# Where a sparse mask is added: by TensorE products, or by VectorE in PSUM from a copy spread through DRAM

## What is computed

```
s = einsum('bqhd,bsd->bqhs', q_idx, k_idx) * (D_IDX ** -0.5)
score = einsum('bqh,bqhs->bqs', w_idx * (H_IDX ** -0.5), relu(s))
score = where(k_pos <= qp, score, -inf)
_, sel = lax.top_k(score, n_sel)          # n_sel = 256, one choice per query, the same for its 8 heads
...
logits = einsum('bqgrd,bqngd->bqgrn', qg, ks) * (DH ** -0.5)
logits = where(valid, logits + bias, -inf)
p = softmax(logits);  o = einsum('bqgrn,bqngd->bqgrd', p, vs)
```

## Time and profile before

| | |
|---|---|
| median of 3 runs | 2370.95 us (2370.91 to 2372.14) |
| the profiled execution's own time | 2371.31 us |
| its span on the core | 2369.8 us |
| TensorE busy | 2354.3 us (99%), 17234 instructions |
| VectorE busy | 1408.5 us (59%) |
| ScalarE busy | 919.7 us (39%) |
| GpSimd busy | 313.1 us (13%) |
| DMA | 458.70 MB, 194 GB/s over the span |
| granted TensorE clock | 0.998 of full speed |

### The profile page before, as it was taken

One profiled execution on the slowest core, in us unless ns is written; L12 is line 12 of the kernel. 1 busy time (PEld: TensorE's weight loads), 2 busy tenths in 40 slices (PEclk: granted clock), 3 DMA queues, 4 the chain that ended last, 5 costly groups with the idle time before them and its releaser, 6 DMA issues.

```text
span 2369.8 us, 44619 instructions
## 1 busy us (share of the span) xinstructions
PE 2354.3 (99%) x17234; PEld 2275.2 (96%) x17242; DVE 1408.5 (59%) x2107; ACT 919.7 (39%) x1283; POOL 313.1 (13%) x629
## 2 busy tenths in 40 slices
PE   9999999999999999999999999999999999999998
PEld 9978999999999999999999999999999999999998
DVE  6535468899987545445456655666654446666443
ACT  5334443433343444444333344333333333333432
POOL 1135110000002322333200011000000000000001
PEclk9999999999999999999999999999999999999999
DMA  7448645556658988999776544444445544444553
GB/s 242 147 131 244 178 148 180 180 169 207 205 174 262 312 291 289 301 334 312 242 264 199 187 152 148 152 154 151 151 148 154 154 151 157 154 149 151 156 149 114
DMA packets 176307, 458.70 MB, mean 194 GB/s; under 512 B 25226, under 2 KB 75002, under 8 KB 175968
## 3 DMA queue, kind: packets, MB, share of 16 engines
q1 hardware_dynamic: 142192, 370.84, 48.6%
q0 software_dynamic: 26128, 75.67, 9.9%
q10 hardware_dynamic: 7776, 9.35, 1.1%
HBM read 425.27 MB, written 27.52 MB: 191 GB/s over the span
## 4 chain that ended last, share of the span: by engine, by line
PE 96%; DVE 1%; ACT 1%; DMA 1%; issue 1%; SPq 0%; DVEq 0%; ACTq 0%
PE ps L803 88%; PE ps L1077 1%; PE ps L1030 1%; PE ps L876 1%; DMA w_raw<-in_w_in 1%; PE ps L1060 1%; ACT w_hi L1129 0%; PE ps L1000 0%; PE ps L943 0%; PE ps L992 0%; PE ps L888 0%; PE ps L979 0%; PE ps L983 0%; DVE w_lo L1406 0%; PE ps L840 0%
## 5 line engine op out<-in xcount | busy, mean ns | idle before, releaser
L1406 DVE TENSOR_TENSOR w_lo<-w_raw,w_hi 128x1024 fp32r<-128x1024 f32 (+2 forms) x630 | 750.8, 1194 | 777.1 <-ACT w_hi L1129 774.0
L803 PE MATMUL ps<-h_hi,w_hi 128*128 128x320 f32 x3696 | 1160.6, 314 | 2.4 <-DVE w_lo L1406 1.2
L803 PE MATMUL ps<-h_lo,w_hi 128*128 128x320 f32 x3696 | 1132.1, 306 | 0.0
L803 PE MATMUL ps<-h_hi,w_lo 128*128 128x320 f32 x3696 | 1125.6, 305 | 0.0
L1129 ACT ACTIVATE w_hi<-w_raw 128x1024 fp32r<-128x1024 f32 (+2 forms) x630 | 649.4, 1033 | 807.0 <-PE ps L803 774.3
L803 PEld LDWEIGHTS ps<-h_hi,w_hi 128*128 128x128 f32 x3696 | 694.5, 188 | 32.5 <-issue 25.7
L803 PEld LDWEIGHTS ps<-h_lo,w_hi 128*128 128x128 f32 x3696 | 694.6, 188 | 0.5
L803 PEld LDWEIGHTS ps<-h_hi,w_lo 128*128 128x128 f32 x3696 | 694.3, 188 | 0.0
L803 PE MATMUL ps<-y_hi,w_hi 128*128 128x320 f32 x688 | 213.3, 310 | 0.0
L803 PE MATMUL ps<-y_lo,w_hi 128*128 128x320 f32 x688 | 210.5, 306 | 0.0
L803 PE MATMUL ps<-y_hi,w_lo 128*128 128x320 f32 x688 | 209.2, 304 | 0.0
(11 more groups left out here) (329 smaller groups left out, 2070.0 us busy)
## 6 DMA issues: line engine op xcount, KB each, us to landing
w_raw<-in_w_in SPq DMA_DIRECT2D x250, 512.0 KB, 5.0
w_raw<-in_ffn_up SPq DMA_DIRECT2D x86, 512.0 KB, 4.0
w_raw<-in_ffn_gate SPq DMA_DIRECT2D x86, 512.0 KB, 3.8
w_raw<-in_ffn_down SPq DMA_DIRECT2D x80, 448.0 KB, 3.4
kpg<-in_cache_b_k SPq DMA_DIRECT2D x128, 128.0 KB, 4.5
vpg<-in_cache_b_v POOLq DMA_DIRECT2D x128, 128.0 KB, 5.1
kpg<-in_cache_a_k SPq DMA_DIRECT2D x128, 128.0 KB, 4.6
vpg<-in_cache_a_v POOLq DMA_DIRECT2D x128, 128.0 KB, 5.0
```

Source lines behind the costliest of these rows:

```text
L803: mm = mmul(bank[q][:, 0:T], wp[:, s, cols], xp[:, x.k0 + k, :], start=(x.first and k == 0 and t == 0), stop=(x.last and k == x.nk - 1 and ...
L1406: tt(w_lo[:, s, 0:n], w_raw[:, s, 0:n], w_hi[:, s, 0:n].bitcast(F32), ALU.subtract).then_inc(w_lo_done, 1)
```

## The change

The mask no longer goes through TensorE. POOL stores `m16` to a DRAM tensor `m_scr` once (at x = 1), and before each pair of mixer A loads it back into the same tile `m16`, now in the order of the logits: for each of the two requests one DMA with the eight rows of its queries repeated over eight heads (64 partitions x 2056). VectorE adds it to the logits in PSUM, one `tensor_tensor` per chunk and one for bank 6. The products with `ecur`, the constant and its load are gone, and so is TensorE's wait for `m16_done`; `lg_ps` comes right after the logits of a chunk. The page table's load now counts on `s_in` with four other constants, and its two waits are for all five. Line numbers in the changed kernel are higher (L1030 becomes L1043, L1039 becomes L1052, L803 becomes L816, L1406 becomes L1407, L1778 becomes L1786, L1795 becomes L1803, L698 becomes L711).

```diff
@@ GpSimd
-            load(ecur[:, :, :], a["c_ecur"].bitcast(BF16), s_in)
...
+            def mask_of(p):
+                for s in range(2):
+                    r = 2 * p + s
+                    row = 32 * (2 * (r % NPAIR % 2) + r // NPAIR) + TS * (r % NPAIR)
+                    load(m16[s * NS:(s + 1) * NS, :], bass.AP(m_scr.tensor, row * L, [[0, H], [L, TS], [1, L]]), m16_moved)
+
             for x in range(2 * NPAIR):
...
-                if x == NPAIR + 1:
+                if x == 1:
                     pool.wait_ge(m16_done, 1)
+                    store(m_scr, m16[:, :], m16_moved)
+                if x == 2:
+                    pool.wait_ge(m16_moved, 16)
+                    mask_of(0)
+                if x > NPAIR:
+                    pool.wait_ge(mx_done, x)
+                    mask_of(x - NPAIR)
@@ TensorE, sample(x)
-                        if mx == 1 and c < 3:
+                        if c < 3:
                             mm.then_inc(lg_ps, 1)
...
-                    if mx == 0:
-                        for c in (2 * two, 2 * two + 1):
-                            mm = mmul(bank[2 + c], ecur[:, p, :], m16[:, c * 512:(c + 1) * 512], start=False, stop=True,
-                                      skip_group_check=True)
-                            if c < 3:
-                                mm.then_inc(lg_ps, 1)
-                        if two == 1:
-                            mm = mmul(bank[6][:, 0:P], ecur[:, p, :],
-                                      m16[:, PAST:L].unsqueeze(1).to_broadcast([P, 2 * NB, TS]),
-                                      start=False, stop=True, skip_group_check=True)
...
-                if x == NPAIR:
-                    pe.wait_ge(m16_done, 1)
@@ VectorE, sample(x)
+                if mx == 0:
+                    dve.wait_ge(m16_moved, 16 + 32 * (p + 1))
                 for c in range(4):
                     dve.wait_ge(lg_ps, 4 * x + c + 1)
+                    if mx == 0:
+                        V(tt(bank[2 + c], bank[2 + c], m16[:, c * 512:(c + 1) * 512], ALU.add))
...
                     if c == 3:
+                        if mx == 0:
+                            of = bank[6][:, 0:P].rearrange("p (b t) -> p b t", t=TS)
+                            V(tt(of, of, m16[:, PAST:L].unsqueeze(1).to_broadcast([P, 2 * NB, TS]), ALU.add))
```

More of the change, by code:

```diff
@@ L170, in build @@
         w_scr = nc.dram_tensor("w_scr", [HI, NS], F32).ap()
+        m_scr = nc.dram_tensor("m_scr", [P, L], BF16).ap()
         sig_scr = nc.dram_tensor("sig_scr", [48, P, T], F32).ap()
@@ L223, in build @@
         nearN = r0("nearN", [P, 2, NPAIR * NB, TS])
-        ecur = r0("ecur", [P, NPAIR, P], BF16)
         od_at = r0.at - R
@@ L358, in build @@
         x_arrived = [sem(f"x_arrived{i}") for i in range(len(X_LOTS))]
-        g_in, ident_in, r_in, idx_in, c_in, pt_in, s_in = (
-            sem(n) for n in ("g_in", "ident_in", "r_in", "idx_in", "c_in", "pt_in", "s_in"))
+        g_in, ident_in, r_in, idx_in, c_in, s_in = (
+            sem(n) for n in ("g_in", "ident_in", "r_in", "idx_in", "c_in", "s_in"))
         eps_set, rounded, split, x_sq, x_sqs, n_sum, n_root, n_rstd = (
@@ L368, in build @@
             sem(n) for n in ("ip_s", "ip_relu", "ip_used", "dn_s", "dn_relu", "dn_w", "sel_done", "m16_done"))
+        m16_moved = sem("m16_moved")
         kix_in = [sem(f"kix_in{i}") for i in range(4)]
@@ L500, in _ @@
             dense(31)
-            sp.wait_ge(pt_in, 16)
+            sp.wait_ge(s_in, 80)
             for i in range(16):
@@ L565, in _ @@
             load(ident[:, :], a["c_ident"], ident_in)
-            load(pt_sb[:, :], a["page_table"].rearrange("(o b) n -> o (b n)", o=1), pt_in)
+            load(pt_sb[:, :], a["page_table"].rearrange("(o b) n -> o (b n)", o=1), s_in)
             for dst, n in ((csel, "c_sel"), (causP, "c_causp")):
@@ L590, in _ @@
             load(qodd[DI:P, :, :], qi[0:DI, :, TP:T], qodd_in)
-            pool.wait_ge(pt_in, 16)
+            pool.wait_ge(s_in, 80)
             for i in range(16):
@@ L1890, in constants @@
     c["c_gmask"] = np.where(np.arange(P)[:, None] % NS // 32 == np.arange(HKV)[None, :], 0, NEG).astype(f)
-    e = (r[:, None, None] == own.T[None, :, :]) & (q[:, None, None] == hq[None, None, :])
-    c["c_ecur"] = np.zeros((P, NPAIR, P), np.uint16)
-    c["c_ecur"][srow] = np.where(e, 0x3F80, 0)
     return {n: np.ascontiguousarray(v) for n, v in c.items()}
```

## The result

The changed kernel takes **2374.97 us** (median of 22 runs, 2370.28 to 2384.35) against 2370.67 us before in the same sessions (22 runs, 2369.56 to 2372.31): a ratio of 1.0018 with a 95% interval of 1.0013 to 1.0024. It is 0.18% slower, where 0.13% faster was forecast, and the time lies above the range. Its times also scatter over 14 us, where those of the kernel before scatter over 3. The profiled execution took 2377.11 us, 2.1 us above the median of the 22, with a span of 2375.6 us, 5.8 us more than the span before.

The account below looks back on a forecast made before the run. TensorE, busy 99% of the span, was taken as the bound. Removed mask products gave -3.15 us; work added to VectorE, POOL and DMA counted 0: 2370.95 - 3.15 = 2367.8 us, range 2366.6 to 2370.3.

Parts of the forecast that it names:

- The bytes: ... I take 0, with 0 to 1.4 us for each of three loads: Mask traffic on the DMA engines: 0.53 MB per load at 375 GB/s, taken as 0, upper bound 4.2 us.
- Weights take 9.1 us to land there, where six units ahead of use are some 20 us: Weight loads in the full DMA stretch: landing in 9.1 us against some 20 us ahead of use, so no cost.
- a row of TensorE's waits for `w_lo`, `pr` or the pages in 975 to 1190: Sign of being wrong: TensorE waiting for these in mixer A's later pairs.
- weights that land more than 10 us later: Sign of failure: weight loads landing more than 10 us later than in the kernel before.
- Rival B: Mask traffic delays weights or pages TensorE takes at once: 2374.8 us for all bytes, 2372.0 for three loads; chance 7%.
- The gain on TensorE: Mask products removed from mixer A's four pairs: 0.787 us a pair, 3.15 us in all, bounds 1.9 and 3.95.
- The 3.7 us worked out from the section "Back-to-back issue gap": Alternative gain on TensorE by the page's cycles: 0.92 us a pair, 3.7 us; the trace's 0.79 was preferred.
- The additions: Mask additions on VectorE: 0.69 us per 512 columns, 12.7 us in all, hidden in idle time, cost 0.
- Its margin: VectorE's room before TensorE asks for the fourth unit's `w_lo`: 6.8 us before, 6.0 us after.
- The masks were in time: Mask loads on POOL's queue: landing 5 to 12 us after issue, 14 us or more before VectorE wants them.
- Rival A: Mask loads land late and VectorE waits, deciding from 21 us to landing: 2378.7 us at 24.2 us; chance 4%.
- C: Rival: VectorE's additions slower than their rows promise and on the path: +9.5 us, 2380.5 us; chance 2%.

Follow-up runs that it names:

- b2_one128: Changed kernel with one mask load of 128 rows into all 128 partitions per pair, in place of two of 64 (wrong rows added): 2368.09 us.
- c1_strided: Changed kernel with a pair's two mask loads each going to every second partition, not spread (wrong rows added): 2367.88 us.
- b3_pe_only: Kernel before without the mask products and with no mask in their place: 2367.17 us.
- a1_tiny: Changed kernel with the mask's store and loads cut to 8 of 2056 columns, all waits, issues and additions kept: 2367.29 us.
- a3_early: Changed kernel with the same mask store and loads issued at other places of POOL's list: 2367.07 us, ratio 0.9983 to the kernel before.
- b4_adds3: a3_early with every mask addition on VectorE made three times: 2377.34 us.
- a2_plain: Changed kernel with each mask load reading 64 successive rows of the copy, none repeated (wrong rows added): 2375.84 us.
- b1_2048: Changed kernel with the mask's DRAM copy and loads cut to 2048 columns, rows of 4096 bytes: 2374.68 us.
- c4_alt: Changed kernel with a pair's mask in four loads of 32 partitions, lower and upper half in turn, correctly spread: 2372.18 us.
- a4: Changed kernel with SP's key page loads all one dense unit earlier, masks where the change put them: 2367.45 us.

## Why the prediction was wrong, step by step

**The step that failed is "The bytes: ... I take 0, with 0 to 1.4 us for each of three loads".** It has two errors, and both are in its own words. First the price: it divides 0.53 MB by the mean rate of the stretch, 375 GB/s. That takes for granted that the mask's bytes move as fast as those which were there. They don't: while the two loads run, everything moves at 205 to 285 GB/s, and the key pages land 3.4 us later in place of 1.4. Second the cover: "Weights take 9.1 us to land there, where six units ahead of use are some 20 us". That is right for `w_raw`, which went to 13.1 us and made TensorE wait nowhere in this stage. But the key pages share SP's queue with the weights, and their cover was never worked out. The rows for it were in the trace of before:

```profile
1021.02 2.54 SPq L473 DMA_DIRECT2D kpg<-in_cache_a_k  x3
```

The last of these three issues begins about 1023.2. The second half of the logits at x = 5 begins one period and 5.87 us after 974.87, at 1033.9, its last chunk 0.85 us later at 1034.7. That is 11.5 us, against a slowest landing of 9.6 us in the stage before: **2 us of room**, where the weights by the same count have some 11 (by the slowest landing of the pages issued in this stretch itself, 8.2 us, it is 3 us). Measured after: issued at 1026.02, wanted at 1037.07, 11.05 us later; landed at 1038.07, after 12.05 us. So 2.85 us of room met a delay of 3.85 us, and the chunk came 1.0 us late.

At x = 2 the landing is only part of it. The page that was waited for is issued at 869.77 and lands after 10.23 us. In the kernel before, the last issue of that pair begins at 867.9 and its pages land after 6.3 us at most. The landing is 3.9 us longer and the issue 1.8 us later, while TensorE itself is 0.5 us later; that uses up the 2.3 us of room there and leaves the 3 us measured. What holds SP's list back by 1.8 us was not looked into.

So the term that was put at 0 measures 10.0 us in the profiled execution, 8.5 of them waits for key pages and 1.5 the lower clock behind one of them. The prediction named "a row of TensorE's waits for `w_lo`, `pr` or the pages in 975 to 1190" as a sign of being wrong, and it came, 4.0 us; the other sign, weights that land more than 10 us later, did not come; it watched the kind of load with the most room.

**Where the loads were counted was too narrow.** Only those for x = 5 to 7 were held to fall where the engines are full. The store at 800.6 and the first load at 853.5 were priced at nothing, and 3.4 of the 7.4 us of waits are behind them: 0.64 behind the store, 2.76 behind the load. The store reads all 128 partitions and is none of the loads of 64; its wait comes and goes between kernels that have the same store (0.6 us in b2_one128, none in c1_strided). In 859 to 862 the engines moved 250 GB/s at a share of 1.05, where they moved 371 before:

```profile
859.00:862.00 3.00, 3.00 (x41) 2.81 (x43) 1.23 (x1) 0.03 (x1) 0.70 (x3) 1.00 1.05 250
```

**Rival B** had the direction and, at its upper end, the size: 2374.8 us against 2374.97. That the numbers meet is luck. It reached its own by all 2.63 MB at 375 GB/s, with every microsecond shown; what happened is more than twice the price, of which 2 to 3 us a pair are covered, with the lower clock on top, and the median it meets is of executions that scatter over 14 us. It got 7% because "TensorE does not wait for a weight or a page anywhere in this stage, although landing doubles there". That a wait is absent says that the room is not used up, not how much is left.

**The gain on TensorE was right.** Forecast 3.15 us from the periods; measured 3.34 (b3_pe_only), 3.42 (a1_tiny) and 3.64 (a3_early). The logits of x = 4 and x = 5, between which nothing waits, begin at 978.35 and 1030.69: 52.34 us, as mixer B. The 3.7 us worked out from the section "Back-to-back issue gap" of the Trainium skill's page "TensorE: Matmul & The Clock Gate" (its cycles for the gap of an isolated matmul) are no worse by these medians, whose intervals span 4 us, while the period of b3_pe_only is decisive for 0.79 us a pair.

**VectorE was right as far as it mattered.** The additions take 0.70 us (0.69 forecast) and 0.30 us, and none was released by a DMA (durations ns min/median/max, first and last start):

```profile
L1772 DVE TENSOR_TENSOR ps<-ps,m x16: 698/699/700, 979.5 to 1149.4; 128x512 f32<-128x512 f32 x16
...
L1779 DVE TENSOR_TENSOR ps<-ps,m x4: 298/300/300, 987.2 to 1150.1; 128x128 f32<-128x128 f32 x4
```

```profile
979.55 0.70 DVE L1772 TENSOR_TENSOR ps<-ps,m 128x512 f32<-128x512 f32 x1 [2.08 <-PE ps L1043]
...
989.37 0.15 DVE L1803 TENSOR_SCALAR stS<-stS 128x1 f32<-128x1 f32 x1
```

The first begins 979.55 - 978.35 = 1.20 us after the logits (1.13 forecast). `mx_done` ends 11.17 us after the logits began, 11.09 before. Its margin was wrong: 4.0 us, not 6.0, since the unit needs a free bank as well as `w_lo`, and I followed `w_lo` alone. In the changed kernel this cost nothing; in b4_adds3 it cost me the expectation.

**The masks were in time**, as forecast: 6.3, 9.3 and 13.4 us to land (min, median, max, the store among them) where 5 to 12 were expected; the slowest, at x = 6, is over that and under the 21 us that would have counted. Rival A did not come about, nor did C. POOL's new waits held nothing up, by a1_tiny.

**The clock** was no term of the sum, and took 1.5 us of the loss (below).

## What to carry to other kernels

Added traffic is priced with the rate that its own shape gets, and its delay is held against the queue's *tightest* customer: issue to use, less the slowest landing, worked out for each kind of load in the queue, not for the largest. If a spread or broadcast load goes to 64 neighbouring partitions, write it over all 128 or every second one, or put it where the pages that follow have room: here the first is worth 7 us and the second 8. The first was measured only with wrong rows of the mask (b2_one128, c1_strided); a right spread in that form was not run. And a change that removes 3 us can only be worth keeping with its transfers placed: a3_early is the change as it was meant, 0.17% faster.

## What the hardware showed that I had not expected

- Two loads of 64 neighbouring partitions, 0.53 MB, pull the rate of all queues together from about 380 to between 205 and 285 GB/s for some 5 us, while the engines count as fully busy; c1_strided with every second partition stays at 393.
- The clock after a wait. TensorE stood for 2.60 us ahead of 1093.26, and then its granted clock was 0.63 of full speed over four microseconds, so partly at its 1.2 GHz level and partly at 2.4:

```profile
1089.00:1093.00 4.00, 1.66 (x13) 0.56 (x11) 2.42 (x4) 1.27 (x2) 2.14 (x4) 1.00 1.04 376
1093.00:1097.00 4.00, 3.74 (x24) 2.71 (x25) 1.91 (x7) 0.25 (x1) 2.15 (x4) 0.63 1.05 376
```

  At x = 2 it stood longer, 2.76 us before 880.04, and kept its 2.4 GHz:

```profile
880.00:884.00 4.00, 3.96 (x35) 3.16 (x36) 2.36 (x9) 0.05 (x1) 2.15 (x4) 1.00 1.04 373
```

  One wait of this length cost 1.5 us more, the other nothing. In the other kernels the clock was lower behind the waits of 3.04 and 2.24 us (a2_plain, 0.76 and 0.66 over the four microseconds from 1036 and from 1146) and of 2.32 us (b1_2048, 0.75 over those from 1142), and stayed full behind those of 1.8 us in c4_alt. Why the one at x = 2 was spared the traces do not tell.
- The changed kernel scatters five times as much as the kernel before. With waits that decide by a microsecond on the landing of one page, each execution can win or lose them anew; that is my reading, from one profile of each kernel. Of the kernels without such a wait, a1, a3, a4 and b3 have ranges of 1.4 to 2.2 us and c1 3.7.
